# A third weight buffer for the expert tiles and deeper loads in the last stage of a hybrid decoder layer

## The chip, the cores and the metric

The kernel runs on all 8 cores of one Trainium2 chip. Each core takes 4 of the 32 sequences, 8192 tokens, and runs the same program on them; nothing is exchanged between cores. The metric is the device time of the slowest core in microseconds.

## The reference

One decoder layer, cut to what matters here:

```python
h = rmsnorm(x, g_mix) * (1.0 + sc1) + sh1
# differential attention (4 heads) beside sliding-window attention (8 heads), one output projection
x = x + gt1 * (concat([o_diff, o_swa]) @ w_out)
h2 = rmsnorm(x, g_ffn) * (1.0 + sc2) + sh2
# 16 experts in 4 groups: the best group, then the best two experts in it, weights in `combine`
for e in range(N_EXPERTS):
    a = silu(h2 @ w_gate[e]) * (h2 @ w_up[e])      # (1024 -> 512)
    y = y + combine[..., e:e + 1] * (a @ w_down[e])  # (512 -> 1024)
x = x + gt2 * y
return rmsnorm(x, g_final)
```

## The kernel before, in words

The kernel has three parts, with a barrier of all engines and DMAs between them.

**Attention and routing.** Projections, both attentions, output projection, second norm and router. It leaves in DRAM `x2d` (the residual stream, float32), `h2d` (the normed input of the experts, bfloat16) and, for each expert, a table of the tokens sent to it. The change leaves this part alone.

**Experts.** The tokens are sorted by expert into 58 tiles of `TS` = 384 rows, which is 3 sub-tiles (`SUB`) of 128. Which expert a tile belongs to is known only at run time, so weights and rows are fetched by gathers that GpSimd (POOL) issues, `K.idma`, line 157: the gate weights `wg`, the up weights `wu` and the down weights `wd` of the tile's expert, 1 MB each, and three gathers of 128 rows of `h2d` into `hg`, 0.25 MB each. For tile i, `b_tr` transposes the rows on TensorE (L1277) into `hgT`, `b_up` computes gate and up products (L1286, L1290) for four column blocks, the transposes of tile i+1 lying between them, and `b_down` computes the down product (L1302). The result, `ysb`, 1.5 MB, is stored to `ysl` by the sync engine (SP). The loop is shifted: turn i does `b_up(i)` and then `b_down(i-1)`. Before, in turn i POOL first issues `load_h(i+2)`, and behind `b_down(i-1)` in the program comes `load_w(i+1)`. `wg`, `wu` and `wd` have two buffers, `hg` three.

The order of the work on each engine is the order of the program. The recording layer `Sched` puts ahead of each instruction the waits for whatever last wrote or read the buffers that it names, and an engine stops at such a wait with all that stands behind it. All three gathers of `load_h` name the same buffer as written:

```python
for s in range(SUB):
    K.idma(hg[s3][:, s, :], None, h2d, gidx[:, i * SUB + s:i * SUB + s + 1], None,
           reads=[b["h2d"], b["gidx"]], writes=[b_hg[s3]])
```

so each of them waits for the landing of the one before it.

**Last stage.** 64 tiles of 128 tokens. `c_load(t)` loads `x2t` from `x2d` (SP) and gathers the two expert results of each token, `y1` and `y2` (POOL). `c_comp(t)` scales `y1` (ScalarE, L1357), combines (VectorE, L1359), multiplies by the gate `G2` (VectorE, L1361), adds to `x2t` (POOL, L1363) and takes the mean square (ScalarE, L1365, then `rstd` at L549 and L550). `c_out(t)` scales into `yo` (VectorE, L1372), and SP stores it to `out`. `NY` = 3 buffers each for `y1`, `y2` and `x2t`, loads two tiles ahead. Ahead of the tiles SP loads `gfin_bc` and the four vectors of `G2`.

Of the kernel before, what the change touches and what calls it, by code (L numbers as in the profile page):

```python
# [11 lines left out]
F32 = mybir.dt.float32  # L12
BF16 = mybir.dt.bfloat16
# [214 lines left out]
def build_nc(NSEQ, S):  # L228
# [61 lines left out]
    with ExitStack() as st:  # L290
# [109 lines left out]
        rC = Region(nc, OW0, OW0 + 48 * KB, "C")  # L400
        gfin_bc = rC.alloc("gfin_bc", [128, D], F32)
        G2 = rC.alloc("G2", [128, NSEQ, D], F32)
        rC2 = Region(nc, rB.off, SB_LIMIT, "C2")
        NY = 3
# [3 lines left out]
        yo = [rC2.alloc(f"yo_{i}", [128, D], F32) for i in range(2)]  # L408
# [42 lines left out]
        b_wg = mkl("wg", 2)  # L451
        b_wu = mkl("wu", 2)
        b_wd = mkl("wd", 2)
        b_hg = mkl("hg", 3)
# [8 lines left out]
        b_yo = mkl("yo", 2)  # L463

        s_mod = [K.new_dma_sem(f"mod{i}") for i in range(2)]
        s_out = [K.new_dma_sem(f"out{i}") for i in range(2)]
# [8 lines left out]
        if True:  # L475
# [995 lines left out]
```

How the kernel before makes its waits and increments, by code:

```python
    def _waits(self, E, deps):  # L87
        for s, v in deps.items():
            if s is E.sem:
                if E.is_pe or v > s.v:
                    continue
            if E.seen.get(s, 0) >= v:
                continue
            assert v <= s.v, f"wait on pending count {E.name} {v} > {s.v}"
            E.q.append(lambda eng, h=s.h, v=v: eng.wait_ge(h, v))
            E.seen[s] = v
# [17 lines left out]
    def op(self, E, fn, reads=(), writes=(), inc=True):  # L114
        fn = _freeze(fn)
        self._waits(E, self._deps(reads, writes))
        if inc:
            E.sem.v += 1
            val = E.sem.v
            E.q.append(lambda eng, fn=fn, h=E.sem.h: fn(eng).then_inc(h, 1))
        else:
            val = E.sem.v + 1
            E.q.append(lambda eng, fn=fn: fn(eng))
        s = E.sem
        for b in reads:
            if b.r.get(s, 0) < val:
                b.r[s] = val
        for b in writes:
            if b.w.get(s, 0) < val:
                b.w[s] = val
# [1 line left out]
    def dma(self, Q, out, in_, sem, reads=(), writes=()):  # L132
        if sem is None:
            wb = writes[0]
            if wb.dsem is None:
                wb.dsem = self.new_dma_sem("d_" + wb.name)
            sem = wb.dsem
        self._waits(Q, self._deps(reads, writes))
        sem.v += 16
        Q.q.append(lambda eng, out=out, in_=in_, h=sem.h: eng.dma_start(out=out, in_=in_).then_inc(h, 16))
        for b in reads:
            b.r[sem] = sem.v
        for b in writes:
            b.w[sem] = sem.v
```

## Time and profile before

| | |
|---|---|
| time, median of 3 runs | 5769.92 us (5699.68 to 5783.97) |
| the profiled execution's own time | 5753.92 us |
| its slowest core's span (core 2) | 5752.4 us |
| spans of the 8 cores | 5634.1 to 5752.4 us |
| PE, DVE, ACT, POOL busy | 3249.9, 1858.0, 1849.5, 1481.2 us |
| mean granted TensorE clock, core 2 | 0.762 |
| moved by DMA | 744.88 MB |

The span runs from the first to the last instruction of the slowest core, and 1.5 us of the execution's time lie outside it. Busy times are sums over parts with different limits, so they do not say what bounds one part.

### The profile page before, as it was taken

How to read it: one execution, taken by the hardware profiler on the slowest of the kernel's cores; microseconds unless marked ns; L12 is line 12 of the kernel's file. 1: busy time of each engine (PE TensorE's matmuls, PEld its weight loads, DVE VectorE, ACT ScalarE, POOL GpSimd, SP SyncE). 2: the span in 40 equal slices, each digit the busy share in tenths (PEclk: the TensorE clock that was granted, in tenths of full speed). 3: DMA queues.
4: the chain of work that ended last, by engine and by line, in shares of the span. 5: the costliest groups of instructions: out<-in, count | busy, mean ns of one | idle time of the engine just before them, and what ended most of it. 6: DMA issues, size and time to landing. Idle time of an engine off the chain costs nothing.

```text
span 5752.4 us, 69188 instructions; the slowest of 8 cores (5634.1 to 5752.4 us)
## 1 busy us (share of the span) xinstructions
PE 3249.9 (56%) x21898; PEld 1766.6 (31%) x21898; DVE 1858.0 (32%) x3753; ACT 1849.5 (32%) x2947; POOL 1481.2 (26%) x1106
## 2 busy tenths in 40 slices
PE   3576637666536666437775656177778777750000
PEld 0143224333224333224442323044444434420000
DVE  0134334334334334334443422121111111114343
ACT  1234353333253343253442422022222222222222
POOL 1111241111331111331213111322222222215555
PEclk7798758887758887768887767589889888875555
DMA  7432252443242343142220132166666666667776
GB/s 156 131 65 43 55 128 68 94 96 62 34 106 76 94 96 65 33 118 70 74 73 18 34 107 101 60 199 229 230 229 230 230 217 222 217 218 232 230 230 209
DMA packets 277509, 744.88 MB, mean 129 GB/s; under 512 B 63392, under 2 KB 113312, under 8 KB 254880
## 3 DMA queue, kind: packets, MB, share of 16 engines
q0 software_dynamic: 113696, 350.46, 23.4%
q1 hardware_dynamic: 163456, 390.00, 20.3%
q8 instruction: 183, 3.00, 0.2%
q14 instruction: 174, 1.43, 0.1%
HBM read 602.84 MB, written 247.63 MB: 148 GB/s over the span
## 4 chain that ended last, share of the span: by engine, by line
PE 29%; DMA 23%; DVE 14%; issue 12%; POOL 9%; ACT 9%; another core or an unknown queue 1%; SPq 1%; DVEq 1%; ACTq 0%; POOLq 0%
DMA B_hg<-h2d,B_gidx 8%; PE ps L729 5%; PE ps L988 4%; DMA wsc_g<-w_gate 4%; DMA B_wu<-wsc_u,B_eidx 4%; POOL C_x2t L1363 3%; PE ps L1290 3%; DMA wsc_u<-w_up 2%; PE ps L1286 2%; PE ps L814 2%; PE ps L1302 2%; POOL A_h2f L1014 2%; DMA Ada_adst<-w_ada 2%; PE ps L697 2%; DVE A_ev L828 2%
## 5 line engine op out<-in xcount | busy, mean ns | idle before, releaser
L795 ACT ACTIVATE A_pT<-ps 128x1024 bf16<-128x1024 f32 (+1 forms) x576 | 553.2, 974 | 297.1 <-PE ps L787 221.8
L814 PE MATMUL ps<-A_dv,A_pT 128*128 128x129 bf16 x4352 | 418.3, 243 | 228.6 <-DVE A_ev L831 197.6
L729 PE MATMUL ps<-A_hT,A_wub 128*128 128x512 bf16 x1664 | 486.3, 445 | 65.6 <-DVE P_stat L826 38.7
L1286 PE MATMUL ps<-B_hgT,B_wg 128*128 128x384 bf16 x1856 | 391.5, 361 | 214.4 <-DMA B_wg<-wsc_g,B_eidx 212.8
L1294 DVE TENSOR_TENSOR B_aT<-ps,B_sg 128x384 bf16<-128x384 f32 x232 | 129.3, 558 | 988.8 <-PE ps L1290 977.7
L814 PEld LDWEIGHTS ps<-A_dv,A_pT 128*128 128x128 bf16 x4352 | 323.5, 108 | 364.3 <-issue 322.1
L1290 PE MATMUL ps<-B_hgT,B_wu 128*128 128x384 bf16 x1856 | 371.2, 347 | 57.1 <-DMA B_wu<-wsc_u,B_eidx 51.4
L157 POOL DMA_INDIRECT B_hg<-h2d,B_gidx x174 | 166.2, 955 | 869.7 <-DMA B_hg<-h2d,B_gidx 819.8
L1302 PE MATMUL ps<-B_wd,B_aT 128*128 128x512 bf16 x1392 | 329.9, 379 | 25.6 <-DVE B_ysb L1308 15.0
L1279 ACT COPY B_hgT<-ps 128x1024 bf16<-128x1024 bf16 x174 | 176.1, 1012 | 433.8 <-PE ps L1277 429.6
L733 DVE TENSOR_TENSOR A_rt<-ps,A_cosb 128x512 f32<-128x512 f32 x208 | 143.8, 691 | 489.7 <-ACT A_qraw L732 376.8
L1014 POOL TENSOR_TENSOR A_h2f<-A_h2f,P_B 128x1024 f32<-128x1024 f32 x64 | 151.0, 2359 | 580.2 <-DVE A_h2f L1012 325.0
L988 PE MATMUL ps<-A_wob,A_oTt 128*128 128x512 bf16 x1024 | 288.9, 437 | 14.7 <-ACT A_h2Tf L1030 6.5
L1286 PEld LDWEIGHTS ps<-B_hgT,B_wg 128*128 128x128 bf16 x1856 | 185.5, 106 | 356.8 <-issue 280.7
L1023 PE MATMUL ps<-P_ident_f,A_h2f 128*128 128x128 f32 x512 | 118.8, 386 | 295.3 <-POOL A_h2f L1014 161.0
L787 PE MATMUL ps<-A_qT,A_kT 64*128 64x256 bf16 (+1 forms) x2304 | 251.5, 302 | 46.5 <-ACT A_pT L795 29.0
L1363 POOL TENSOR_TENSOR C_x2t<-C_x2t,C_y 128x1024 f32<-128x1024 f32 x64 | 206.8, 3230 | 244.2 <-DVE C_y L1361 225.5
L729 PEld LDWEIGHTS ps<-A_hT,A_wub 128*128 128x128 bf16 x1664 | 170.1, 110 | 310.1 <-issue 205.1
L549 ACT ACTIVATE P_stat<-P_stat,P_epsc 128x1 f32<-128x1 f32 (+1 forms) x320 | 94.4, 295 | 516.4 <-DVE A_evj L835 478.3
L1290 PEld LDWEIGHTS ps<-B_hgT,B_wu 128*128 128x128 bf16 x1856 | 186.2, 102 | 217.1 <-issue 114.5
L745 POOL TENSOR_TENSOR A_qT<-A_rt,A_rt 128x512 bf16<-128x512 f32 x64 | 85.4, 1335 | 642.9 <-DVE A_rt L744 518.3
L659 POOL TENSOR_TENSOR A_hb<-A_h2f,P_B 128x1024 bf16<-128x1024 f32 x64 | 153.7, 2412 | 375.3 <-DVE A_h2f L657 231.6
(174 smaller groups left out, 5319.9 us busy)
## 6 DMA issues: line engine op xcount, KB each, us to landing
ysl<-B_ysb SPq DMA_DIRECT2D x58, 1536.0 KB, 10.2
A_xs<-x SPq DMA_DIRECT2D x128, 512.0 KB, 4.2
x2d<-A_xs SPq DMA_DIRECT2D x64, 512.0 KB, 2.7
C_x2t<-x2d SPq DMA_DIRECT2D x64, 512.0 KB
out<-C_yo SPq DMA_DIRECT2D x64, 512.0 KB, 2.8
Ada_adst<-w_ada SPq DMA_DIRECT2D x12, 2048.0 KB, 12.7
A_wub<-wsc_in SPq DMA_DIRECT2D x32, 512.0 KB, 4.1
wsc_g<-w_gate POOLq DMA_DIRECT2D x16, 1024.0 KB, 19.0
```

The source lines that it names most:

```text
L157: Q.q.append(lambda eng, h=sem.h: eng.indirect_dma_start(out=out, out_offset=oo, in_=in_, in_offset=io).then_inc(h, 16))
L729: K.op(PE, lambda e, k=k: e.matmul(bank(pbi), lhsT=w[:, k, col * 128:(col + 1) * 128], rhs=hT[:, k, j * 512:(j + 1) * 512], start=(k == 0) ...
L787: K.op(PE, lambda e: e.matmul(ps[st2][:, o_], lhsT=k_[rows, c * 128:(c + 1) * 128], rhs=q_[rows, q0:(j + 1) * 256], start=True, stop=True) ...
L795: K.op(ACT, lambda e: e.activation(out=dst, in_=src, func=AF.Exp, scale=0.125), reads=[PB[2 * st2], PB[2 * st2 + 1]], writes=[bp])
L814: K.op(PE, lambda e: e.matmul(bank(4 + q2)[:, m * 129:(m + 1) * 129], lhsT=pt[:, o0:o0 + 128], rhs=dv[:, c, h, :], start=(pr == 0 and ci = ...
L988: K.op(PE, lambda e, kk=kk: e.matmul(bank(pbi), lhsT=oTt[d2][:, kk, :], rhs=wob[:, kk, half * 512:(half + 1) * 512], start=(kk == 0), stop ...
L1014: K.op(POOL, lambda e: e.tensor_tensor(out=h2f[hs][:], in0=h2f[hs][:], in1=B2[:], op=ALU.add), reads=[b_h2f[hs], b["B2"]], writes=[b_h2f[hs]])
L1279: K.op(ACT, lambda e: e.copy(out=hgT[s2][:, :, s * 128:(s + 1) * 128], in_=pv.rearrange("p (k c) -> p k c", k=8)), reads=[PB[pbi]], writes ...
L1286: K.op(PE, lambda e, k=k: e.matmul(bank(gb)[:, 0:TS], lhsT=wg[s2][:, k * 512 + m * 128:k * 512 + (m + 1) * 128], rhs=hgT[s2][:, k, :], sta ...
L1290: K.op(PE, lambda e, k=k: e.matmul(bank(ub)[:, 0:TS], lhsT=wu[s2][:, k * 512 + m * 128:k * 512 + (m + 1) * 128], rhs=hgT[s2][:, k, :], sta ...
L1302: K.op(PE, lambda e, m=m: e.matmul(bank(yb), lhsT=aT[s2][:, m, s * 128:(s + 1) * 128], rhs=wd[s2][:, m * 1024 + half * 512:m * 1024 + (hal ...
L1363: K.op(POOL, lambda e: e.tensor_tensor(out=x2t[n][:], in0=x2t[n][:], in1=y2[n][:], op=ALU.add), reads=[b_x2t[n], b_y2[n]], writes=[b_x2t[n]])
```

## The change

`wg`, `wu` and `wd` get a third buffer each and `hg` a fourth. `load_w` is split: `load_gu` (gate and up) and `load_d` (down). In turn i POOL now issues `load_h(i+3)`, then `load_gu(i+2)`, then, behind `b_down(i-1)` in the program, `load_d(i+2)`. The loads ahead of the first turn stand in another order. In the last stage there are five buffers for `y1`, `y2` and `x2t` and three for `yo`, and the loads run four tiles ahead. To make room, the last stage's tensors now lie over those of the expert part (the barrier stands between).

```diff
-        wg = [rB.alloc(f"wg{i}", [128, 4096], BF16) for i in range(2)]
-        wu = [rB.alloc(f"wu{i}", [128, 4096], BF16) for i in range(2)]
-        wd = [rB.alloc(f"wd{i}", [128, 4096], BF16) for i in range(2)]
-        hg = [rB.alloc(f"hg{i}", [128, SUB, D], BF16) for i in range(3)]
+        wg = [rB.alloc(f"wg{i}", [128, 4096], BF16) for i in range(3)]
+        wu = [rB.alloc(f"wu{i}", [128, 4096], BF16) for i in range(3)]
+        wd = [rB.alloc(f"wd{i}", [128, 4096], BF16) for i in range(3)]
+        hg = [rB.alloc(f"hg{i}", [128, SUB, D], BF16) for i in range(4)]
...
-        NY = 3
+        NY = 5
...
-            def load_w(i):
-                s2 = i % 2
-                for dst, wb, tab in ((wg, b_wg, wsc_g), (wu, b_wu, wsc_u), (wd, b_wd, wsc_d)):
-                    K.idma(dst[s2][:], None, tab.rearrange("e p n -> (e p) n"), eidx[:, i:i + 1], None,
-                           reads=[b["eidx"]] + b_wsc, writes=[wb[s2]])
+            def load_gu(i):
+                s3 = i % 3
+                for dst, wb, tab_ in ((wg, b_wg, wsc_g), (wu, b_wu, wsc_u)):
+                    K.idma(dst[s3][:], None, tab_.rearrange("e p n -> (e p) n"), eidx[:, i:i + 1], None,
+                           reads=[b["eidx"]] + b_wsc, writes=[wb[s3]])
+
+            def load_d(i):
+                s3 = i % 3
+                K.idma(wd[s3][:], None, wsc_d.rearrange("e p n -> (e p) n"), eidx[:, i:i + 1], None,
+                       reads=[b["eidx"]] + b_wsc, writes=[b_wd[s3]])
...
-            load_w(0)
             load_h(0)
-            load_w(1)
+            load_gu(0)
             load_h(1)
+            load_d(0)
+            load_gu(1)
+            load_d(1)
+            load_h(2)
             for s in range(SUB):
                 b_tr(0, s)
             for i in range(NTILE + 1):
                 if i < NTILE:
+                    if i + 3 < NTILE:
+                        load_h(i + 3)
                     if i + 2 < NTILE:
-                        load_h(i + 2)
+                        load_gu(i + 2)
                     for m in range(4):
                         b_up(i, m)
                         if m < SUB and i + 1 < NTILE:
...
-                    if i + 1 < NTILE:
-                        load_w(i + 1)
+                if i + 2 < NTILE:
+                    load_d(i + 2)
...
-            c_load(0)
-            c_load(1)
+            for t in range(NY - 1):
+                c_load(t)
             for t in range(NTT + 1):
                 if t < NTT:
                     c_comp(t)
                 if t >= 1:
                     c_out(t - 1)
-                if t + 2 < NTT:
-                    c_load(t + 2)
+                if t + NY - 1 < NTT:
+                    c_load(t + NY - 1)
```

POOL in the middle of the expert part, before: one turn of its queue, from one down load to the next. `s79_pe` counts TensorE's steps, and `d_wd0`, `d_hg2` and their like count the landings in that buffer.

```order
L157 DMA B_wd0_127<-wsc_d,B_eidx_147 128x4096 [waits s91_d_wd0,s79_pe]
L157 DMA B_hg2_131<-h2d,B_gidx_156 128x1024 [waits s97_d_hg2] x3
L157 DMA B_wg1_124<-wsc_g,B_eidx_147 128x4096 [waits s93_d_wg1]
L157 DMA B_wu1_126<-wsc_u,B_eidx_147 128x4096 [waits s94_d_wu1]
L157 DMA B_wd1_128<-wsc_d,B_eidx_147 128x4096 [waits s95_d_wd1,s79_pe]
```

And the same place after the change, where TensorE's counter is `s80_pe`:

```order
L157 DMA B_wd0_129<-wsc_d,B_eidx_151 128x4096 [waits s94_d_wd0,s80_pe]
L157 DMA B_hg1_133<-h2d,B_gidx_160 128x1024 [waits s93_d_hg1] x3
L157 DMA B_wg2_125<-wsc_g,B_eidx_151 128x4096 [waits s100_d_wg2]
L157 DMA B_wu2_128<-wsc_u,B_eidx_151 128x4096 [waits s101_d_wu2]
L157 DMA B_wd2_131<-wsc_d,B_eidx_151 128x4096 [waits s102_d_wd2,s80_pe]
```

Nothing moves within the turn: the kinds of loads, their order and the kinds of their waits are the same. What differs is the tile that each is for, and so how old the step of TensorE is that the down load waits for: `b_down(i-1)` for the weights of tile i+1 before, for those of tile i+2 now.

POOL at the start of the expert part, before:

```order
L157 DMA B_wg0_123<-wsc_g,B_eidx_147 128x4096
L157 DMA B_wu0_125<-wsc_u,B_eidx_147 128x4096
L157 DMA B_wd0_127<-wsc_d,B_eidx_147 128x4096
L157 DMA B_hg0_129<-h2d,B_gidx_156 128x1024 [waits s81_dve]
L157 DMA B_hg0_129<-h2d,B_gidx_156 128x1024 [waits s92_d_hg0] x2
L157 DMA B_wg1_124<-wsc_g,B_eidx_147 128x4096
```

and after the change:

```order
L157 DMA B_hg0_132<-h2d,B_gidx_160 128x1024 [waits s82_dve]
L157 DMA B_hg0_132<-h2d,B_gidx_160 128x1024 [waits s90_d_hg0] x2
L157 DMA B_wg0_123<-wsc_g,B_eidx_151 128x4096
L157 DMA B_wu0_126<-wsc_u,B_eidx_151 128x4096
L157 DMA B_hg1_133<-h2d,B_gidx_160 128x1024
L157 DMA B_hg1_133<-h2d,B_gidx_160 128x1024 [waits s93_d_hg1] x2
```

The rows of the first tile now go out ahead of its weights, and its down weights behind the rows of the second tile.

## Rows read from the trace of the kernel before

**Rows 1.** Busy time by stretch: the three parts, then two steady stretches, core 2.

```profile
0.00:3692.00 3692.00, 2137.92 (x15400) 1172.96 (x15400) 1361.74 (x3121) 1283.58 (x2045) 821.10 (x566) 0.76 0.32 78
3692.00:5141.00 1449.00, 1111.95 (x6498) 593.67 (x6498) 258.98 (x440) 392.70 (x581) 331.51 (x349) 0.88 0.63 221
5141.00:5752.40 611.40, 0.00 (x0) 0.00 (x0) 237.24 (x192) 173.18 (x321) 328.59 (x192) 0.50 0.72 224
3800.00:5000.00 1200.00, 932.08 (x5442) 495.79 (x5440) 209.80 (x341) 327.78 (x487) 278.76 (x293) 0.89 0.64 226
4563.00:4576.00 13.00, 10.16 (x62) 5.48 (x61) 1.81 (x3) 3.44 (x6) 1.90 (x2) 0.87 0.96 363
4576.00:4584.00 8.00, 7.85 (x50) 4.28 (x49) 1.93 (x4) 2.83 (x5) 2.62 (x3) 1.00 0.18 45
```

**Rows 2.** Who waited for whom, 3800 to 5000 us: total us, times, longest.

```profile
PE ps L1286 <- DMA B_wg<-wsc_g,B_eidx: 199.9, 44, 12.6
PE ps L1290 <- DMA B_wu<-wsc_u,B_eidx: 46.1, 43, 2.2
...
POOL B_hg L157 <- DMA B_hg<-h2d,B_gidx: 704.0, 93, 14.6
POOL B_wd L157 <- PE ps L1302: 130.4, 36, 7.3
```

**Rows 3.** POOL in order of time, one turn without a wait for TensorE.

```profile
3855.41 0.95 POOL L157 DMA_INDIRECT B_wg<-wsc_g,B_eidx  x1 [0.30 <-issue]
3856.67 0.95 POOL L157 DMA_INDIRECT B_wu<-wsc_u,B_eidx  x1 [0.30 <-issue]
3857.92 0.94 POOL L157 DMA_INDIRECT B_wd<-wsc_d,B_eidx  x1 [0.30 <-issue]
3859.16 0.96 POOL L157 DMA_INDIRECT B_hg<-h2d,B_gidx  x1 [0.30 <-issue]
3873.01 0.96 POOL L157 DMA_INDIRECT B_hg<-h2d,B_gidx  x1 [12.89 <-DMA B_hg<-h2d,B_gidx]
3879.68 0.95 POOL L157 DMA_INDIRECT B_hg<-h2d,B_gidx  x1 [5.71 <-issue]
3880.93 0.95 POOL L157 DMA_INDIRECT B_wg<-wsc_g,B_eidx  x1 [0.30 <-issue]
```

**Rows 4.** POOL in order of time, one turn with a long wait for TensorE.

```profile
4171.93 0.95 POOL L157 DMA_INDIRECT B_wg<-wsc_g,B_eidx  x1 [0.30 <-issue]
...
4181.38 0.94 POOL L157 DMA_INDIRECT B_wd<-wsc_d,B_eidx  x1 [7.25 <-PE ps L1302]
...
4193.72 0.96 POOL L157 DMA_INDIRECT B_hg<-h2d,B_gidx  x1 [10.14 <-DMA B_hg<-h2d,B_gidx]
```

**Rows 5.** POOL in order of time: the last unstalled turn's ends, and two lone row gathers.

```profile
4984.30 0.95 POOL L157 DMA_INDIRECT B_wg<-wsc_g,B_eidx  x1 [0.30 <-issue]
...
5008.43 0.95 POOL L157 DMA_INDIRECT B_wg<-wsc_g,B_eidx  x1 [0.30 <-issue]
...
3725.52 0.96 POOL L157 DMA_INDIRECT B_hg<-h2d,B_gidx  x1 [7.71 <-DMA B_hg<-h2d,B_gidx]
3729.60 0.95 POOL L157 DMA_INDIRECT B_hg<-h2d,B_gidx  x1 [3.13 <-DMA B_hg<-h2d,B_gidx]
```

**Rows 6.** POOL: the fourth gate load of the part and the 57th (weights of tiles 3 and 56).

```profile
3780.02 0.95 POOL L157 DMA_INDIRECT B_wg<-wsc_g,B_eidx  x1 [0.30 <-issue]
...
5080.24 0.95 POOL L157 DMA_INDIRECT B_wg<-wsc_g,B_eidx  x1 [0.30 <-issue]
```

**Rows 7.** All engines in order of time, one turn of the last stage.

```profile
5409.45 1.29 DVE L1359 SCALAR_TENSOR_TENSOR C_y<-C_y,P_cw,C_y 128x1024 f32<-128x1024 f32 x1 [5.31 <-ACT C_y L1357]
5412.21 3.25 POOL L1363 TENSOR_TENSOR C_x2t<-C_x2t,C_y 128x1024 f32<-128x1024 f32 x1 [3.52 <-DVE C_y L1361]
...
5415.61 1.06 ACT L1365 ACTIVATE C_junk<-C_x2t 128x1024 bf16<-128x1024 f32 x1 [6.26 <-POOL C_x2t L1363]
5417.34 1.13 ACT L1357 ACTIVATE C_y<-C_y,P_cw 128x1024 f32<-128x1024 f32 x1
5418.58 1.28 DVE L1359 SCALAR_TENSOR_TENSOR C_y<-C_y,P_cw,C_y 128x1024 f32<-128x1024 f32 x1 [5.32 <-ACT C_y L1357]
```

**Rows 8.** SP and POOL in order of time, the start of the last stage.

```profile
5141.47 17.95 SPq L140 DMA_DIRECT2D C_G<-mod_scr  x4
...
5165.29 2.33 POOL L1363 TENSOR_TENSOR C_x2t<-C_x2t,C_y 128x1024 f32<-128x1024 f32 x1 [18.69 <-DMA C_x2t<-x2d]
```

More of the change, by code:

```diff
@@ L398, in build_nc @@
         sli = rB.alloc("sli", [128, 2, NTT], I32)
[L400 to L403, printed above, removed]
-        NY = 3
+        rC2 = Region(nc, OW0, rB.off - 4 * NTT * 2, "C2")
+        gfin_bc = rC2.alloc("gfin_bc", [128, D], F32)
+        G2 = rC2.alloc("G2", [128, NSEQ, D], F32)
+        NY = 5
         y1 = [rC2.alloc(f"y1_{i}", [128, D], F32) for i in range(NY)]
@@ L407, in build_nc @@
         x2t = [rC2.alloc(f"x2t_{i}", [128, D], F32) for i in range(NY)]
-        yo = [rC2.alloc(f"yo_{i}", [128, D], F32) for i in range(2)]
+        yo = [rC2.alloc(f"yo_{i}", [128, D], F32) for i in range(3)]
         junk3 = rC2.alloc("junk3", [128, D], BF16)
@@ L450, in build_nc @@
         b_wsci = mkl("wsci", len(WBLK))
[L451 to L454, printed above, removed]
+        b_wg = mkl("wg", 3)
+        b_wu = mkl("wu", 3)
+        b_wd = mkl("wd", 3)
+        b_hg = mkl("hg", 4)
         b_hgT = mkl("hgT", 2)
@@ L462, in build_nc @@
         b_x2t = mkl("x2t", NY)
-        b_yo = mkl("yo", 2)
+        b_yo = mkl("yo", 3)
         s_mod = [K.new_dma_sem(f"mod{i}") for i in range(2)]
-        s_out = [K.new_dma_sem(f"out{i}") for i in range(2)]
+        s_out = [K.new_dma_sem(f"out{i}") for i in range(3)]
         s_wc = [K.new_dma_sem(f"wc{i}") for i in range(NE)]
@@ L1276, in b_tr @@
                 for k in range(8):
-                    K.op(PE, lambda e, k=k: e.transpose(out=pv[:, k * 128:(k + 1) * 128], in_=hg[s3][:, s, k * 128:(k + 1) * 128], identity=ident_b[:]),
-                         reads=[b_hg[s3], b["ident_b"]], writes=[PB[pbi]], inc=(k == 7))
+                    K.op(PE, lambda e, k=k: e.transpose(out=pv[:, k * 128:(k + 1) * 128], in_=hg[s4][:, s, k * 128:(k + 1) * 128], identity=ident_b[:]),
+                         reads=[b_hg[s4], b["ident_b"]], writes=[PB[pbi]], inc=(k == 7))
                 K.op(ACT, lambda e: e.copy(out=hgT[s2][:, :, s * 128:(s + 1) * 128], in_=pv.rearrange("p (k c) -> p k c", k=8)),
@@ L1297, in b_down @@
             def b_down(i, s):
-                s2 = i % 2
+                s2, s3 = i % 2, i % 3
                 for half in range(2):
@@ L1302, in b_down @@
                         K.op(PE, lambda e, m=m: e.matmul(bank(yb), lhsT=aT[s2][:, m, s * 128:(s + 1) * 128],
-                                                         rhs=wd[s2][:, m * 1024 + half * 512:m * 1024 + (half + 1) * 512],
+                                                         rhs=wd[s3][:, m * 1024 + half * 512:m * 1024 + (half + 1) * 512],
                                                          start=(m == 0), stop=(m == 3)),
-                             reads=[b_aT[s2][m], b_wd[s2]], writes=[PB[yb]], inc=(m == 3))
+                             reads=[b_aT[s2][m], b_wd[s3]], writes=[PB[yb]], inc=(m == 3))
                     ysv = ysb[s2][:, s, half * 512:(half + 1) * 512]
@@ L1371, in c_out @@
                 ssap = stat[:, 12 + d2:13 + d2]
-                K.op(DVE, lambda e: e.scalar_tensor_tensor(out=yo[d2][:], in0=x2t[n][:], scalar=ssap, in1=gfin_bc[:],
+                K.op(DVE, lambda e: e.scalar_tensor_tensor(out=yo[t % 3][:], in0=x2t[n][:], scalar=ssap, in1=gfin_bc[:],
                                                            op0=ALU.mult, op1=ALU.mult),
-                     reads=[b_x2t[n], b_st[4 + d2], b["gfin_bc"]], writes=[b_yo[d2]])
-                K.dma(SP, out[t // NT, (t % NT) * 128:(t % NT + 1) * 128, :], yo[d2][:], s_out[d2], reads=[b_yo[d2]])
-            c_load(0)
-            c_load(1)
+                     reads=[b_x2t[n], b_st[4 + d2], b["gfin_bc"]], writes=[b_yo[t % 3]])
+                K.dma(SP, out[t // NT, (t % NT) * 128:(t % NT + 1) * 128, :], yo[t % 3][:], s_out[t % 3], reads=[b_yo[t % 3]])
+            for t in range(NY - 1):
+                c_load(t)
             for t in range(NTT + 1):
```

16 lines of the change are left out of this document (8 added, 8 removed).

## The prediction

> **What bounds the kernel now.** I read the stretches first, to see how much of the span the change can touch. The attention part takes 3692 us and is not changed; the experts take 1449 us and the last stage 611 us [rows 1]. What matters in these two is which wait ends last.
>
> *Experts.* The list of waits shows TensorE waiting for the gate weights, 199.9 us in 44 waits of a 1200 us stretch, and 46.1 us for the up weights [rows 2]. That invites the reading "the loads are too late, issue them earlier". But the reader should look at who issues them. On POOL, over the same 1200 us, 704.0 us are spent waiting for the landing of row gathers, and 130.4 us (36 waits) for TensorE's down product [rows 2]. All six loads of a tile go through POOL's one queue, in the order down weights, three gathers, gate, up; each gather waits for the one before it, and the gate load stands behind all three. One turn of this queue that waits for TensorE nowhere looks so [rows 3]: gate to first gather 3.75 us (three issues), first to second gather 13.85 us, second to third 6.67 us, third to the next gate 1.25 us; 25.52 us in all. The second gather comes late because the first is queued behind 3 MB of weights.
>
> So the expert part is bounded by a loop through POOL's queue and the landing of gathers. How often it turns is read from its gate loads: tile 3's at 3780.02 and tile 56's at 5080.24, 1300.2 us for 53 turns, 24.53 us each [rows 6]. TensorE is busy for 932.08 of 1200 us, so about 19.1 us of a turn [rows 1]. Nor do the DMA engines fill the turn: in the burst behind the weight issues they are 0.96 busy at 363 GB/s, and in the 8 us in which POOL waits for the later gathers 0.18 busy at 45 GB/s [rows 1].
>
> *Last stage.* One turn is 5409.45 to 5418.58, 9.13 us [rows 7]: VectorE to the start of POOL's add 2.76 us, the add 3.40 us, ScalarE's mean square and root 1.73 us, its scaling of the next tile's `y1` 1.24 us. The four steps close the loop with no DMA in it: ScalarE's `y1` scaling of tile t+1 stands behind the root of tile t in its own queue, and it starts as soon as that is done. The loads are in time already with two tiles ahead.
>
> **The change part by part.** The sum is made against the profiled execution, 5753.9 us.
>
> *Third weight buffer, weights a tile earlier.* It removes POOL's wait for TensorE: the down load now waits for a down product that ended a whole turn earlier. TensorE's wait for the gate weights does not go with it, for the queue turns no faster than its gathers allow, and TensorE, with 19.1 us of work per turn, catches up with whatever lead it has and waits for each gate load again. So the price is POOL's turn without the TensorE wait. The trace has such turns: of the 54 turns between 3751 and 5080 us ten had no such wait, the first at 3855.41 (25.52 us) [rows 3], the last 4984.30 to 5008.43 (24.13 us) [rows 5]; the shortest took 22.6 us, the mean is 23.7 us. The gain is less than the wait removed (130.4 us in the 1200 / 24.53 = 49 turns of that stretch, 2.66 us each), because in a stalled turn the DMA engines go on with gate and up weights: the turn with the longest stall but two, 7.25 us, reached its second gather 21.8 us after the gate load [rows 4], the unstalled one 17.6 us after [rows 3], so 7.25 us of stall cost 4.2 us; and stalls under 4 us cost next to nothing (mean over these turns 17.8 us from gate load to second gather, against 17.1 us over the ten). I take 24.53 - 23.66 = 0.87 us a turn (the 23.7 averaged with a straight line through all 54 turns, which gives 23.65 at no stall), times 53 = 46 us. The bounds: the whole stall comes back, 2.66 x 53 = 141 us; or none of it, because the burst merely runs into busy engines sooner.
>
> *Fourth row buffer, rows three ahead.* They never were awaited by TensorE in the steady stretch: no such wait is in the list [rows 2]. Worth nothing; the wait of one gather for the next within `load_h` stays (the order after the change shows it), and with it the 704 us.
>
> *Order at the start.* The first tile's rows go ahead of its weights. Two lone gathers stand 4.08 us apart [rows 5], so rows 0 take 3 x 4.1 us, and TensorE starts some 6 us sooner. Walking the queue on at the row's prices, the gate load of tile 3 comes at about 3777, against 3780.0 [rows 6]: the same number of gathers and weights must pass either way. 0 to -3 us; I take 0. At the end nothing changes: behind the last gathers the remaining weights go out at once in both kernels.
>
> *Last stage, loads four ahead, five buffers.* The loop has no load in it, so 0 us in the steady turns. At the start two more tiles' gathers (4 x 0.5 MB) share the engines with the chain of `G2` loads, 17.95 us long, on which the first add waits at 5165.29 [rows 8]. 2.1 MB at the burst's 363 GB/s is 6 us of DMA time, but part of that chain is latency. Between 0 and +6 us; I take +2. The third `yo` buffer: the store's place on SP is not waited for; 0.
>
> Sum: -46 + 2 = -44 us, so 5710 us in an execution like the profiled one. The median of the runs shown lies 16 us above the profiled time; from it, 5770 - 44 = **5726 us**.
>
> The Trainium skill, page "DMA: Bandwidth & Descriptors", section Specifications, gives a core about 358 GB/s of HBM when its neighbour streams too. A turn moves 3 x 1.05 MB of weights, 0.79 MB of rows and a store of 1.57 MB, 5.5 MB, so by that rule the transfers need an estimated 15.4 us and would let TensorE set the pace (the second rival). The trace shows bursts of 363 GB/s but a mean of 226 GB/s [rows 1]: no run here shows that this limit is what holds the turn.
>
> The same page, section "Anatomy of one DMA", puts a GpSimd-issued transfer at 2.0 us + bytes / 436e3, an estimated 2.6 us for a gather of 0.25 MB; the row says 4.1 us for a lone one [rows 5]. By the page's price a turn would be about 1.5 us shorter in both kernels, and the difference between them the same.
>
> **The rivals.**
>
> *The whole stall comes back.* If the burst is limited by when POOL hands over its loads and not by the engines, a turn is 24.53 - 2.66 = 21.9 us: 5770 - 141 + 2 = 5631 us. For it: turns as short as 22.6 us occur. Against it: in the burst the engines are 0.96 busy.
>
> *TensorE sets the pace.* If the lead of two tiles did hide the gathers, a turn would be TensorE's 19.1 us: 53 x 5.4 = 288 us, 5484 us. For it: the list of TensorE's waits. Against it: a third buffer makes nothing in POOL's queue shorter, and 704 us of gather waits remain.
>
> *No gain at all.* The stalls vanish but the first gather lands no sooner, since the engines were full: 5770 us. For it: short stalls cost nothing even now. Also a case in which the change does not do what it says: TensorE waits for the gate weights as before.
>
> *Slower.* POOL now issues weights and first gather in one go each turn, and SP's 1.5 MB store falls into the burst every time, which in the unstalled turns of today it only does in part. The place is the wait of the second gather. It decides against the change once the mean unstalled turn passes 24.53 us; two of the ten had 25.5. At 25.5 in all turns: +0.97 x 53 = 51 us, 5823 us.
>
> **How the numbers follow.** Forecast 0.58; whole stall 0.14; TensorE's pace 0.06; no gain 0.15; slower 0.07. The range has to leave out no more than 2 in 10: from the whole stall's 5630 to 5785, which takes in no gain and part of the slower case; outside lie TensorE's pace and the rest. About 2%, 115 us, is what a measurement of this kernel can tell from no change. Faster by more than that is TensorE's pace and nearly all of the whole-stall case, 0.19; slower by more than that takes an unstalled turn beyond 26.7 us, 0.04; within it 0.77.
>
> **What the changed profile would show.** POOL's wait of the down load for L1302 gone; its waits for gathers still about 700 us of 1200, perhaps a little more; TensorE's wait for gate weights still there, 4 us or more a turn; the turn 23.7 us; the mean DMA rate up from 226 to 234 GB/s; the last stage at 9.13 us a turn, its first add up to 6 us later. I am wrong if the gather waits shrink (then what held them was not the queue of weights ahead of them), if TensorE's gate wait is gone, or if the last stage's turn changes at all.

## The result and the profile after

| | median, us | lowest to highest | runs |
|---|---|---|---|
| before | 5766.3 | 5699.7 to 5828.2 | 16 |
| after | 5669.7 | 5643.8 to 5733.1 | 16 |

The ratio is 0.9865, with a 95% interval of 0.9831 to 0.9899: the change takes off 78 us, between 58 and 97. The profiled execution took 5652.4 us, its slowest core 2 5650.8 us. Forecast were a gain of 44 us and a range of 5630 to 5785, so direction and range held and the gain was larger than the sum. In some executions of any kernel one die is a per cent or more behind the other; the ratios, and the differences in us worked out from them, leave these out on both sides, and where too few are left for a ratio the text gives the median of those left and their number, so that a ratio can differ from the quotient of two medians.

The view of the cores (span, mean granted TensorE clock) has to be read first, because this execution shows two kinds of core.

```profile
core 2: 5650.8 us, clock 0.693
...
core 5: 5593.2 us, clock 0.769
...
die 0 (median of its cores): 5624.2 us, clock 0.696
die 1 (median of its cores): 5607.3 us, clock 0.769
```

Cores 0 to 3 had a lower clock than cores 4 to 7 and spans of nearly the same length. Core 5 can be set beside the cores of before at nearly the same clock (0.92 in the stretch below, 0.89 before); core 2 can't, and is shown beside it. Here are 1100 us of the expert part on both, by stretch (busy us of PE, PEld, DVE, ACT, POOL, then the granted clock, the DMA share and GB/s), core 5 first, then core 2:

```profile
3800.00:4900.00 1100.00, 882.98 (x5231) 472.04 (x5229) 201.47 (x328) 315.51 (x467) 268.24 (x282) 0.92 0.68 233
...
3800.00:4900.00 1100.00, 1052.55 (x5587) 554.42 (x5636) 214.24 (x353) 332.97 (x502) 285.70 (x301) 0.80 0.73 251
```

Then who waited for whom in that stretch (total us, times, longest), core 5 after:

```profile
POOL B_hg L157 <- DMA B_hg<-h2d,B_gidx: 754.1, 89, 15.8
...
PE ps L1290 <- DMA B_wg<-wsc_g,B_eidx: 159.2, 46, 9.6
...
PE ps L1294 <- DMA B_wu<-wsc_u,B_eidx: 39.6, 40, 1.9
...
POOL B_wd L157 <- issue: 12.7, 47, 0.3
```

and core 2 after, whose list has no wait of TensorE (PE) for weights at all, the largest wait of its matmuls being the second line here:

```profile
POOL B_hg L157 <- DMA B_hg<-h2d,B_gidx: 705.7, 94, 12.8
...
PE ps L1306 <- DVE B_ysb L1312: 38.4, 25, 3.1
```

and core 5 before, which [rows 2] show for core 2 over 1200 us:

```profile
POOL B_hg L157 <- DMA B_hg<-h2d,B_gidx: 654.7, 87, 13.9
...
PE ps L1286 <- DMA B_wg<-wsc_g,B_eidx: 181.5, 40, 12.4
...
POOL B_wd L157 <- PE ps L1302: 121.4, 32, 7.5
```

The wait that the change was expected to remove, 121.4 us of POOL for the down product, is gone: the down load waits only 0.3 us of issue each time. In its place the waits for row gathers grew by 99 us. On core 5, as on cores 4, 6 and 7, TensorE still waits for gate weights, and everything goes as before, only 0.7 us a turn sooner. On cores 0 to 3 it does not wait for them any more: on core 2 it is busy for 1052.55 of 1100 us, 21.05 us of a turn of 22.00. POOL in order of time, core 5, one turn, beside [rows 3] and [rows 4]:

```profile
4139.22 0.95 POOL L157 DMA_INDIRECT B_wg<-wsc_g,B_eidx  x1 [0.27 <-issue]
4140.43 0.95 POOL L157 DMA_INDIRECT B_wu<-wsc_u,B_eidx  x1 [0.27 <-issue]
4141.65 0.94 POOL L157 DMA_INDIRECT B_wd<-wsc_d,B_eidx  x1 [0.27 <-issue]
4142.87 0.95 POOL L157 DMA_INDIRECT B_hg<-h2d,B_gidx  x1 [0.27 <-issue]
4154.56 0.95 POOL L157 DMA_INDIRECT B_hg<-h2d,B_gidx  x1 [10.74 <-DMA B_hg<-h2d,B_gidx]
4160.39 0.95 POOL L157 DMA_INDIRECT B_hg<-h2d,B_gidx  x1 [4.87 <-DMA B_hg<-h2d,B_gidx]
```

The list of loads has changed, the loop has not: three weight loads and a gather at intervals of 1.2 us, then a gather that waits for the one before it, then another. From the gate loads of tiles 3 and 56 the turn is, before, 24.32 to 24.73 us on the eight cores (mean 24.46); after, 23.60 to 23.84 us on cores 4 to 7 (mean 23.72, forecast 23.66), and 21.47 to 22.04 us on cores 0 to 3 (mean 21.76).

Core 5 of the two profiled executions, part by part, in us:

| core 5 | before | after | difference |
|---|---|---|---|
| up to the gate load of tile 3 | 3668.2 | 3667.5 | -0.7 |
| 53 turns | 1291.0 | 1250.9 | -40.1 |
| from tile 56's to the last stage | 62.8 | 59.6 | -3.2 |
| last stage | 612.9 | 615.2 | +2.3 |
| span | 5634.9 | 5593.2 | -41.7 |

On this core that is the forecast sum of -44 nearly term by term; the 53 turns of cores 4, 6 and 7 took 43, 33 and 29 us less. Core 2 took 132 us off its 53 turns, began them 15.4 us later and lost 9.9 us behind them and 5.6 us in the last stage: 101.6 us in all.

### The profile page after: what moved, and what is told of

Read it like the earlier page. It is cut to its first block, busy times and chain, and to the rows that moved or that the text cites. A ratio compares the mean times of both kernels' runs of the same rounds, so it can differ in the third digit from the quotient of the medians.

```text
span 5650.8 us, 68965 instructions; the slowest of 8 cores (5584.3 to 5650.8 us)
## 1 busy us (share of the span) xinstructions
PE 3491.5 (62%) x21656; PEld 1878.0 (33%) x21898; DVE 1861.5 (33%) x3753; ACT 1847.0 (33%) x2947; POOL 1480.9 (26%) x1106
## 3 DMA queue, kind: packets, MB, share of 16 engines
q0 software_dynamic: 113696, 350.46, 22.9%
## 4 chain that ended last, share of the span: by engine, by line
PE 45%; DVE 13%; issue 11%; DMA 11%; ACT 8%; POOL 8%; another core or an unknown queue 1%; SPq 1%; DVEq 1%; ACTq 0%; POOLq 0%
PE ps L1306 7%; PE ps L1290 6%; PE ps L1294 6%; PE ps L728 6%; PE ps L987 4%; DMA wsc_g<-w_gate 3%; POOL C_x2t L1372 3%; PE ps L813 3%; PE ps L696 2%; DMA wsc_u<-w_up 2%; PE ps L786 2%; POOL A_h2f L1013 2%; DMA Ada_adst<-w_ada 2%; PE ps L1034 2%; PE ps L1281 2%
## 5 line engine op out<-in xcount | busy, mean ns | idle before, releaser
L813 PE MATMUL ps<-A_dv,A_pT 128*128 128x129 bf16 x4352 | 447.5, 256 | 256.6 <-DVE A_ev L830 164.1
L728 PE MATMUL ps<-A_hT,A_wub 128*128 128x512 bf16 x1549 | 506.0, 481 | 69.5 <-DVE P_stat L825 21.3
L813 PEld LDWEIGHTS ps<-A_dv,A_pT 128*128 128x128 bf16 x4352 | 348.6, 115 | 356.3 <-issue 349.0
L1306 PE MATMUL ps<-B_wd,B_aT 128*128 128x512 bf16 x1335 | 392.0, 449 | 57.6 <-DVE B_ysb L1312 49.8
L1294 PE MATMUL ps<-B_hgT,B_wu 128*128 128x384 bf16 x1856 | 408.5, 373 | 4.1 <-DVE B_aT L1298 4.1
L1290 PE MATMUL ps<-B_hgT,B_wg 128*128 128x384 bf16 x1856 | 409.4, 373 | 1.4 <-ACT B_hgT L1283 1.4
L987 PE MATMUL ps<-A_wob,A_oTt 128*128 128x512 bf16 x991 | 305.5, 464 | 17.7 <-ACT A_h2Tf L1029 6.8
L786 PE MATMUL ps<-A_qT,A_kT 64*128 64x256 bf16 (+1 forms) x2304 | 267.4, 319 | 44.0 <-ACT A_pT L794 24.6
L1294 PEld LDWEIGHTS ps<-B_hgT,B_wu 128*128 128x128 bf16 x1856 | 202.6, 109 | 170.2 <-issue 9.1
L1290 PEld LDWEIGHTS ps<-B_hgT,B_wg 128*128 128x128 bf16 x1856 | 195.4, 109 | 144.1 <-issue 22.8
```

The source lines that it names most:

```text
L728: K.op(PE, lambda e, k=k: e.matmul(bank(pbi), lhsT=w[:, k, col * 128:(col + 1) * 128], rhs=hT[:, k, j * 512:(j + 1) * 512], start=(k == 0) ...
L786: K.op(PE, lambda e: e.matmul(ps[st2][:, o_], lhsT=k_[rows, c * 128:(c + 1) * 128], rhs=q_[rows, q0:(j + 1) * 256], start=True, stop=True) ...
L813: K.op(PE, lambda e: e.matmul(bank(4 + q2)[:, m * 129:(m + 1) * 129], lhsT=pt[:, o0:o0 + 128], rhs=dv[:, c, h, :], start=(pr == 0 and ci = ...
L987: K.op(PE, lambda e, kk=kk: e.matmul(bank(pbi), lhsT=oTt[d2][:, kk, :], rhs=wob[:, kk, half * 512:(half + 1) * 512], start=(kk == 0), stop ...
```

## The experiments

My theory before the runs: POOL's queue of gather landings sets the turn, and all of the gain is the removed wait of the down load. Against it stood that TensorE's lead of two tiles does the work, that the last stage gives some of it, and, for the cores with short turns, that something else moved.

**1. The expert part alone.** The changed kernel with the last stage's three input buffers, two `yo` buffers and loads two ahead.

```diff
-        NY = 5
+        NY = 3
```

> The changed kernel with the last stage as before (three buffers, loads two tiles ahead). Theory (the last stage's loop has no load in it): time within 10 us of the changed kernel, so about 75 us under the kernel before; the last stage turns in 9.1 us. Rival (the deeper loads of the last stage gave part of the gain): 20 us or more slower than the changed kernel.

5659.6 us (7 runs) against 5740.1 (18 runs of before on this chip); ratio 0.9894, interval 0.9852 to 0.9936, so -61 us. Turns 23.49 us on cores 4 to 7 and 22.38 on cores 0 to 3, which again had a lower clock over the whole kernel (0.73; between 3800 and 4900 us cores 0 and 1 had 0.92 and 0.94, cores 2 and 3 had 0.81). The gain is there without the last stage. The 75 us expected can't be told from 61, since the interval reaches from 37 to 85 us.

**2. The last stage alone.** The kernel before with five input buffers, three `yo` buffers and loads four ahead.

> The kernel before with only the last stage changed (five buffers, loads four tiles ahead). Theory: 0 to +6 us against the kernel before; expert turn 24.5 us, last-stage turn 9.1 us. Rival (the last stage gives 20 us or more of the gain): faster than before by that much.

5739.2 us (12 runs), ratio 0.9987, interval 0.9941 to 1.0034, which is -34 to +20 us. VectorE's combine in the last stage, core 5, as a group (duration min/median/max in ns, first and last start):

```profile
L1358 DVE SCALAR_TENSOR_TENSOR C_y<-C_y,P_cw,C_y x44: 1284/1285/1286, 5201.4 to 5594.8; 128x1024 f32<-128x1024 f32 x44
```

44 of them from 5201.4 to 5594.8: 393.4 / 43 = 9.15 us a turn, against 9.13 [rows 7]. Two more tiles of lead are worth nothing in the turn.

**3. One buffer alone.** The kernel before, its order of loads untouched, with a third buffer for the down weights.

```diff
-        wd = [rB.alloc(f"wd{i}", [128, 4096], BF16) for i in range(2)]
+        wd = [rB.alloc(f"wd{i}", [128, 4096], BF16) for i in range(3)]
```

> The kernel before with a third buffer for the down weights alone; gate and up weights keep two buffers and their place, rows too. Theory (the gain comes from GpSimd no longer waiting for TensorE at the down load, and not from loads being issued earlier): GpSimd's wait for the down product goes to nearly 0 and the expert turn falls to 23.7 us, 40 to 80 us less than before, as in the whole change. Rival (the distance of the gate and up loads matters): the turn stays at 24.5 us.

5672.0 us (6 runs), ratio 0.9891, interval 0.984 to 0.9942: -63 us, the same as all of the expert change. The gate loads on POOL and two waits, 3800 to 4900 us, core 5:

```profile
L157 POOL DMA_INDIRECT B_wg<-wsc_g,B_eidx x47: 947/951/953, 3815.9 to 4896.7; - x47
```

```profile
PE ps L1286 <- DMA B_wg<-wsc_g,B_eidx: 143.0, 43, 7.5
...
POOL B_wd L157 <- issue: 13.5, 47, 0.7
```

1080.8 / 46 = 23.50 us a turn (mean of the eight cores 23.40, granted clock 0.91 to 0.93 in this stretch). TensorE's lead of two tiles, the third gate and up buffers and the fourth row buffer add nothing that these runs show: what paid is that a load with free space behind it no longer stops POOL's queue.

**4. The gathers apart.** In the changed kernel the three gathers of a tile write into one buffer with one semaphore, and so each waits for the one before. Here each slice has its own.

```diff
-        b_hg = mkl("hg", 4)
+        b_hg = [mkl(f"hg{i}_", SUB) for i in range(4)]
...
-  ... writes=[b_hg[s4]])
+  ... writes=[b_hg[s4][s]])
```

> The changed kernel with each of the three row gathers of a tile recorded as a buffer of its own, with its own semaphore, so that a gather no longer waits for the one before it. Theory (GpSimd's loop of gather landings sets the turn): the turn falls to TensorE's pace, 18 to 21 us, and TensorE waits for no weights; 100 to 250 us less than the changed kernel. Rival (the DMA engines or HBM set the turn): the turn stays above 22.5 us and TensorE goes on waiting for gate weights.

5458.8 us (6 runs), ratio 0.9409 (3 of the 6 runs), interval 0.9348 to 0.9469, so -339 us against before and, beside the change's ratio of 0.9865, which was measured against other runs of before, some 260 us beyond it: the largest effect of a single edit. POOL in order of time, core 0:

```profile
4200.13 0.94 POOL L157 DMA_INDIRECT B_wd<-wsc_d,B_eidx  x1 [10.38 <-PE ps L1306]
4201.37 0.96 POOL L157 DMA_INDIRECT B_hg<-h2d,B_gidx  x1 [0.30 <-issue]
4202.64 0.96 POOL L157 DMA_INDIRECT B_hg<-h2d,B_gidx  x1 [0.30 <-issue]
4203.90 0.95 POOL L157 DMA_INDIRECT B_hg<-h2d,B_gidx  x1 [0.30 <-issue]
4205.16 0.95 POOL L157 DMA_INDIRECT B_wg<-wsc_g,B_eidx  x1 [0.30 <-issue]
4206.41 0.95 POOL L157 DMA_INDIRECT B_wu<-wsc_u,B_eidx  x1 [0.30 <-issue]
4217.74 0.94 POOL L157 DMA_INDIRECT B_wd<-wsc_d,B_eidx  x1 [10.37 <-PE ps L1306]
```

All six loads now go out at intervals of 1.25 us, and POOL waits for TensorE: 17.6 us from one down load to the next. By stretch, core 0, columns as above:

```profile
3850.00:4450.00 600.00, 586.97 (x3813) 332.89 (x3811) 146.35 (x238) 229.97 (x341) 194.56 (x205) 1.00 0.99 312
```

TensorE is busy for 587 of 600 us and the DMA engines for 0.99 of them at 312 GB/s: both full at once. The turn is 17.9 to 18.6 us on six cores and 20.6 us on cores 4 and 5. The profiled execution of experiment 12, which has the same expert part, has 17.9 to 18.5 us on all eight, so the 20.6 is not put down to the edit.

**5. The same edit in the kernel before.**

> The kernel before (two weight buffers, three row buffers) with the three row gathers of a tile recorded as buffers of their own, so that none waits for the one before. Theory (the wait of gather for gather is what sets the turn, and the distance of the loads is worth little beside it): the turn falls from 24.5 to between 18 and 21 us, 180 to 300 us less than before, near what the changed kernel reached with the same edit (5459 us); TensorE waits for weights no more, or little. Rival (distance is needed as well): it gains less than 100 us, and TensorE goes on waiting for gate weights.

5537.9 us (2 of 4 runs) against 5744.3 (7 runs): -206 us, inside the 180 to 300 expected, though on two runs only. Turns of 19.8 to 21.2 us, and TensorE's waits for gate weights on core 5 are down to 8.8 us of 900. The waits, core 5, 3800 to 4700 us:

```profile
POOL B_wd L157 <- PE ps L1302: 585.5, 43, 17.6
...
PE ps L1290 <- issue: 37.9, 64, 2.0
```

Here the wait that the change removes is back as the main one, 13.6 us each. With the gathers apart the change's buffers and order are worth some 130 us (339 less 206, on two chips and few runs), against 61 to 78 without: the turn goes from 19.8 to 21.2 us down to 17.9 to 18.6. A lead of two tiles pays once the queue is not held by gathers.

**6, 7, 8. The store moved.** Theory after the first runs: on the cores with short turns TensorE ends its turn later, so SP's 1.5 MB store of `ysb` goes out behind the burst of weights and not in it. To test this on cores at the higher clock, the store of tile i - 2 was issued behind the gate and up product of block m of tile i, with m = 2, 0 and 1.

```diff
+                        if m == 2 and i >= 2:
+                            store(i - 2, [b_aT[i % 2][2]])
```

> The changed kernel with the store of a tile's result held back until the third column block of the next turn is done, some 18 us after the gate load, when POOL waits for the later gathers. Theory of the store's place (the first gather lands late when the 1.5 MB store runs beside the burst of weights, which would explain why the cores at the lower clock turned faster): on cores at the full clock, gate load to second gather falls from 16.5 to 15 us or less, the turn from 23.7 to 22.5 us or less. Rival (the store's place does not matter, something else made those cores faster): 23.3 us or more.

> The control to the run before: the same edit, but the store is held back only to the first column block of the next turn, some 11 us after the gate load, in the burst. Theory of the store's place: no gain, 23.3 us or more a turn. Rival (holding the store back helps in itself): as fast as the other.

> The changed kernel with the store held back to the second column block of the next turn, some 14 to 15 us after the gate load, just when the second gather goes out, as it lies on the cores at the lower clock. Theory of the store's place: this is the best place, a turn of 22.5 us or less (22.75 with the third block, 23.1 with the first, 23.7 unchanged). Rival (the clock or TensorE's waits explain those cores): 22.8 us or more.

m = 2: 5665.9 us (2 of 4 runs) against 5744.3 (7 runs), turns 22.50 to 23.09 (mean 22.75). m = 0: 5689.6 us (4 runs), ratio 0.9878, interval 0.9773 to 0.9984, turns 22.93 to 23.25 (mean 23.11). m = 1: 5643.2 us (5 runs), ratio 0.9819, interval 0.9757 to 0.9882, turns 20.9 to 21.3 on cores 4 to 7 and 21.5 to 22.5 on cores 0 to 3. So m = 1 came in under the 22.5 us of the theory, and m = 2 and m = 0 lie between theory and rival. By their times none of the three can be told from the changed kernel (ratio 0.9865); what they show, they show in the turn. The gate loads of m = 1, core 5:

```profile
L157 POOL DMA_INDIRECT B_wg<-wsc_g,B_eidx x47: 941/951/954, 3816.2 to 4766.0; - x47
```

949.8 / 46 = 20.65 us. The lower bound of 23.3 expected for m = 0 was missed, and how is instructive. As a control it was not placed as meant: the store went out some 13 us behind the gate load, and not 11. On core 5 it took 13.9 us from the gate load to the second gather (m = 1: 13.9 as well), but from the second gather to the third 7.9 us (m = 1: 5.9). The store had not become free, it had moved from one gather to the next.

**9. TensorE made slower.** The other test of the same theory: the changed kernel, the 16 gate and up matmuls of block 3 done twice with the same values, some 2.6 us more TensorE work a turn.

```diff
+                for q_ in range(2 if m == 3 else 1):
+                    for k in range(8):
```

> The changed kernel with more work for TensorE: the 16 matmuls of the fourth column block are done twice (same values), 2.6 us more a turn at full clock, so TensorE alone takes 20.5 us, as it does on the cores at the lower clock. Theory (a slower TensorE lets the store fall behind the burst, and keeps it from catching up with the gate load): the turn falls from 23.7 to 22.5 us or less at the full clock, TensorE's wait for gate weights falls to under a third, and the kernel is faster, or no slower, for doing more. Rival (those cores were faster for another reason): the turn stays at 23.3 us or more.

5611.6 us (4 runs) against 5748.0, ratio 0.9775, interval 0.972 to 0.983: doing more did not cost anything, and -129 us is more than the change's own -78 (whose interval, 0.9831 to 0.9899 against other runs of before, lies just beside this one). The granted clock was 0.98 to 0.99 on all eight cores between 3800 and 4900 us; cores 0 to 3 turned in 22.0 to 22.5 us, as the theory had it, and cores 4 to 7 in 22.6 to 22.9, between theory and rival. TensorE's wait for gate weights is in no list of cores 0 to 3 and 50.8 us on core 5, under a third of 159.2. The gate loads of core 0 (3800 to 4900 us), then the stretch:

```profile
L157 POOL DMA_INDIRECT B_wg<-wsc_g,B_eidx x50: 947/954/955, 3818.7 to 4892.1; - x50
```

```profile
3800.00:4900.00 1100.00, 1013.54 (x6333) 569.68 (x6383) 212.87 (x349) 332.73 (x499) 286.24 (x300) 0.98 0.72 251
```

21.91 us a turn at a granted clock of 0.98, as on core 2 of the changed kernel at 0.80. So the lower clock is not needed for the short turn; a longer TensorE turn at the higher clock brings it too, and with it the store goes out later. SP in order of time shows where the store goes out. Core 5 of the changed kernel, in the turn shown above:

```profile
4145.43 0.36 SPq L140 DMA_DIRECT2D ysl<-B_ysb  x1
```

6.2 us behind the gate load at 4139.22. And core 2, POOL and then SP:

```profile
4134.29 0.95 POOL L157 DMA_INDIRECT B_wg<-wsc_g,B_eidx  x1 [0.30 <-issue]
...
4147.40 0.96 POOL L157 DMA_INDIRECT B_hg<-h2d,B_gidx  x1 [8.40 <-DMA B_hg<-h2d,B_gidx]
4152.98 0.95 POOL L157 DMA_INDIRECT B_hg<-h2d,B_gidx  x1 [4.61 <-DMA B_hg<-h2d,B_gidx]
```

```profile
4150.44 0.36 SPq L140 DMA_DIRECT2D ysl<-B_ysb  x1
```

16.2 us behind it, after the first gather has landed. Over all turns between 3800 and 4900 us:

| core of a kernel | granted clock | store behind gate load, us (mean) | gate load to second gather | turn |
|---|---|---|---|---|
| before, core 5 | 0.89 | 4.9 | 17.8 | 24.32 |
| after, core 5 | 0.92 | 4.8 | 16.6 | 23.64 |
| third down buffer alone, core 5 | 0.91 | 5.5 | 16.4 | 23.49 |
| more matmuls, core 5 | 0.99 | 7.7 | 15.9 | 22.86 |
| expert part alone, core 2 | 0.81 | 8.6 | 15.0 | 21.75 |
| store behind m = 0, core 5 | 0.93 | 13.3 | 13.9 | 23.05 |
| after, core 2 | 0.80 | 15.9 | 14.5 | 22.00 |
| more matmuls, core 0 | 0.98 | 15.7 | 14.2 | 21.91 |
| store behind m = 1, core 5 | 0.94 | 15.8 | 13.9 | 20.65 |
| store behind m = 2, core 5 | 0.94 | 17.6 | 15.6 | 22.19 |

With the store some 5 us behind the gate load the second gather comes 16.4 us or more after it; with the store 15 us behind, 14.5 us or less, and the turn is about 2 us shorter. At 13.3 us the store goes out just as the first gather lands and holds up the second. With m = 2 it goes out at anything from 0.1 to 24.9 us, in some turns beside the next turn's weights, and part of the gain is lost.

The store does not have to leave the burst, though, and the clock alone does not do it. The changed kernel and experiments 1, 10 and 11 have the same expert part; their profiled executions hold 1686 turns with one store in each, here sorted by the store's place and by the granted clock over the turn:

| store behind gate load, us | turns | turn at a clock of 0.86 or more | turn below 0.86 |
|---|---|---|---|
| 4 to 6 | 456 | 23.8 | 23.8 |
| 6 to 8 | 336 | 23.0 | 22.9 |
| 8 to 12 | 296 | 22.0 | 21.9 |
| 12 to 14 | 55 | 23.2 | 22.7 |
| 14 to 18 | 310 | 23.0 | 21.7 |

A store 8 to 12 us behind the gate load, ahead of the first gather's landing, already has the short turn, at either clock. Further out the two clocks part, for a reason that is not known. This is a sorting of turns and not an experiment; the experiment is m = 1.

**10. The last stage's loop cut.** In the changed kernel `c_comp` was split, so that POOL's add of tile t, the scaling and combine of tile t + 1, and the mean square of tile t follow in that order.

```diff
             for t in range(NTT + 1):
                 if t < NTT:
-                    c_comp(t)
+                    c_add(t)
+                if t + 1 < NTT:
+                    c_comp(t + 1)
+                if t < NTT:
+                    c_sq(t)
```

> The changed kernel, the last stage written in another order: the scaling, combining and gating of tile t+1 stand ahead of the mean square of tile t, so that the loop VectorE, GpSimd, ScalarE, ScalarE is cut; five buffers, loads four ahead. Theory (the turn of the last stage is a chain of four engines' steps with no load in it): it falls from 9.1 to 6 to 7 us, 130 to 190 us less in all. Rival (the loads bound it): it stays above 8.5 us.

5520.5 us (4 runs), ratio 0.9598, interval 0.9548 to 0.9649: -231 us, some 150 beyond the change. POOL's add, core 0, 5200 to 5450 us:

```profile
L1374 POOL TENSOR_TENSOR C_x2t<-C_x2t,C_y x38: 2342/2698/3249, 5199.8 to 5443.9; 128x1024 f32<-128x1024 f32 x38
```

244.1 / 37 = 6.60 us a turn in this stretch, 6.28 to 6.43 over the stage on the eight cores, against 9.13 before and 9.15 after the change. The loop named in the prediction was what held this stage.

**11. The same with three buffers,** two of `yo`, loads two ahead.

> The last stage interleaved as in the run before it (6.4 us a turn with five buffers), but with three buffers and loads two tiles ahead; experts as in the changed kernel. Theory: once the compute loop is cut, the distance of the loads counts. A tile's gathers (2.5 us to issue, 5.6 us to land), scaling and combining (3.7 us) and add (3.3 us) then fill two turns, so 7.5 us a turn, 7 to 8.3; 50 to 100 us slower than with five buffers. Rival (two tiles ahead is enough in any order): 6.4 to 6.7 us.

5579.0 us (4 runs), ratio 0.9707, interval 0.9642 to 0.9772; a turn of 7.36 to 7.81 us (expected 7.5). The wait for loads, core 0, same stretch, here and under it with five buffers:

```profile
ACT C_y L1365 <- DMA C_y<-ysl,B_sli: 146.2, 33, 6.8
```

```profile
ACT C_y L1365 <- DMA C_y<-ysl,B_sli: 80.9, 38, 3.8
```

4.4 us a turn against 2.1 us. The change's deeper loads are worth 1.2 us a turn (7.57 less 6.35 as means of the eight cores), 78 us over 64 tiles, but only after the loop is cut; the two medians, from two chips, stand 59 us apart.

**12. Both together:** the gathers apart and the loop cut.

> The changed kernel with both edits: the row gathers recorded apart, and the last stage interleaved. Expected from their sum: 5459 - 150 = about 5300 us, 5220 to 5350. If the two shared a limit, over 5400 us.

5182.0 us (1 of 6 runs, the profiled one) against 5743.7 (8 of 11 runs), outside the 5220 to 5350 expected on the low side, with turns of 17.9 to 18.5 us and a last-stage turn of 6.2 to 6.3 us. The five other runs took 5350.9 to 5396.1 us, so no ratio is given and the size of the gain is open. The two turns are those of experiments 4 and 10: the two edits share no limit that shows there.

## Why the prediction was right, and what it mis-sized

*What bounds the experts: right on cores 4 to 7.* The loop through POOL's queue and the gather landings. The gather waits were to stay at some 700 us of 1200 "perhaps a little more"; on core 5 they went from 654.7 to 754.1 us of 1100, by 15%. TensorE's gate wait stayed, 159.2 us in 46 waits, 3.4 us a turn where 4 us or more was expected. Cutting the gather waits gave 339 us against before, where the change gave 78. The reading that the prediction warned of ("loads are too late, issue them earlier") is refuted, as the cause of this gain, by the third run: loads at the old distance and one more down buffer do the same. On cores 0 to 3 one of the prediction's own signs of being wrong came true: "if TensorE's gate wait is gone". At a granted clock of 0.80 TensorE had 21.05 us of work in a turn of 22.00, where the prediction counted on 19.1 for every core, and it no longer caught up with its weights. These cores ran close to the rival "TensorE sets the pace", at a lower clock than the one for which its 19.1 us were read.

*The price of the removed wait: right near the clock for which it was worked out.* 23.66 forecast, 23.72 measured on cores 4 to 7; of the 2.66 us of stall these cores got 0.68 back (24.40 to 23.72), with 0.87 forecast. It was read from turns of before that happened to have no stall, and so already held whatever the burst runs into. That it came within 0.1 us is luck in part: the ten turns run from 22.6 to 25.5 us. The DMA rate was to rise from 226 to 234 GB/s; on core 5 it rose from 228 to 233.

*Row buffer, start, last stage: right.* The gate load of tile 3 stands 88.5 us behind the last step of the preparation before and 89.8 us after, on core 2; on the eight cores the difference runs from -6.8 to +3.7 us, with a mean of -0.1 where 0 was taken. The last stage's turn went from 9.13 to 9.15 us. Its start came later on core 2 than taken: the chain of `G2` loads took 22.07 us, not 17.95 [rows 8]. SP and then POOL, core 2:

```profile
5033.87 0.35 SPq L140 DMA_DIRECT2D C_gfin_bc<-g_fin  x1
5034.27 22.07 SPq L140 DMA_DIRECT2D C_G<-mod_scr  x4
```

```profile
5062.24 2.33 POOL L1372 TENSOR_TENSOR C_x2t<-C_x2t,C_y 128x1024 f32<-128x1024 f32 x1 [17.80 <-DMA C_x2t<-x2d]
```

The first add comes 28.4 us after the stage's first load, against 24.2 before: +4 us on this core and +2.5 as the mean of the eight, where +2 was taken out of 0 to +6.

*The term that was mis-sized: the turn after the change, 0.87 us a turn times 53.* The step is "I take 24.53 - 23.66 = 0.87 us a turn": it took one length of turn for all cores, and on cores 0 to 3 of the profiled execution the turn fell by 2.5 to 3.0 us. It rests on turns of core 2 before, and there the store went out less than 11 us behind the gate load in every turn between 3800 and 4900 us; the text mentions the store only in the slower rival, as something that would then fall "into the burst every time", and not as something that might leave it. Without POOL's stall the store's place depends on how long TensorE's turn is. Where it went out later, turns were 21.5 to 22.0 us, the length of the rival "the whole stall comes back" (21.9), but by another mechanism: that rival said that POOL's hand-over limits the burst, and at the store's old place the stall did not come back (23.72). The direct move (m = 1: 20.65 us on core 5, where TensorE was busy for 866 of 1100 us and its pace did not bind) shows that the store's place shortens the turn; the added matmuls (21.91 at a clock of 0.98) agree.

*What stays open.* How much of the measured 78 us the store accounts for. In the profiled execution the cores with short turns gained 132 to 158 us in the 53 turns and were still the later ones (5624.2 us against 5607.3 as medians of the two dies): core 2 began the part 15 us later and lost as much behind it. The cause of these was not looked for. The six executions with all cores at the higher clock, in which by this account only the forecast 44 us were to be expected, have a median near 5662 us, no higher than the rest, which speaks against the store's place on cores at the lower clock as the source of all that the sum missed; none of them was profiled. So the mis-sized term is shown for the turn, and not for the time. Tile 3's gate load comes at 3664.5 to 3780.0 us on the eight cores of before, over 100 us apart, and the metric is the slowest core; the runs of the expert part alone and of the third buffer alone (-61 and -63) have intervals that reach from the forecast to the measured value.

The Trainium skill, page "DMA: Bandwidth & Descriptors", section Specifications, was weighed in the prediction for its rate of 358 GB/s a core and the rival that came of it (TensorE's pace). Neither kernel ran near it, at 226 and 233 GB/s; with the gathers apart the engines were busy for 0.99 of the time at 312 GB/s on core 0, and no core of any profiled execution had more than 313 between 3850 and 4450 us.

## What to carry to other kernels

When an engine waits for a DMA, ask who issues that DMA and what stands ahead of it in the issuer's queue: several gathers into one buffer with one semaphore waited for one another, and a semaphore for each took off 206 us by itself and some 260 us on top of the deeper buffers, which by themselves took off 78. A deeper buffer pays only where the loop it feeds is bound by loads: in the last stage nothing before the loop of four engines was cut, 1.2 us a turn after. And when a turn's price is read from rows, look at what else lies in all of those rows (here a store of 1.5 MB in the burst), since the change may move that too.

## What was not expected of the hardware

- A store of 1.5 MB on the other queue, going out during a burst of 3 MB of weight loads and a gather, went with a landing of the gather some 2.7 us later than one going out 11 us after that (16.6 us on core 5 of the changed kernel against 13.9 with the store behind m = 1, from gate load to second gather).
- More TensorE work made the kernel no slower and the turn shorter (from 23.7 to between 22.0 and 22.9 us), while that store went out 3 to 11 us later.
- The granted clock was 1.00 on a core whose TensorE was busy for 587 of 600 us, and 0.80 on a core with 1052.55 of 1100 us busy, in another execution; what decides was not found.
- With the gathers apart in the kernel before, TensorE on core 5 made pauses of up to 2.0 us ahead of matmuls of one line for which no releaser is shown (L1290, 37.9 us in 64 pauses of 900 us); the cause is not known.
- GpSimd's add of 128x1024 f32 in the last stage of the kernel before, core 2, took 2.33 us the one time that no VectorE instruction ran beside it, and 3.19 to 3.25 us the 63 times that one did, for about 1 us each.
